# Who writes the second copy of the keys: two engines or two transfers

## The chip, the cores and the metric

The kernel runs on one core of one Trainium2 chip. The metric is the device time of one execution in microseconds (us), lower is better. Before the change the median of three runs is 1610.96 us (1610.89 to 1611.48).

## The reference, cut to what matters

Two layers of a streaming encoder (512 tokens, width 2048, everything float32). Each layer normalises `x`, projects it by one large matrix, and runs two attentions side by side:

```
h = rmsnorm(x, norm_g)
aq, ak, av, ag, bq, bk, bv, bg = split(h @ w_in)
ya = chunk_relbias_attention(aq, ak, av, rel_bias) * silu(ag)   # mixer A: 16 heads of 64, relative bias
yb = swa_sink_gqa(rope(bq), rope(bk), bv, sinks) * silu(bg)     # mixer B: 16 query heads, 2 key heads
x  = x + concat([ya, yb]) @ w_out
```

A last `rmsnorm` follows. In both mixers the scores are `q . k` over a head's 64 numbers.

## The kernel before, in words

Float32 products are made of three products of a faster format: each operand is split into a high part (`hi`, a rounding copy on ScalarE, helper L1110) and a low part (`lo`, the difference, on VectorE, helper L1581/L1582), and PE adds hi x hi, lo x hi and hi x lo (L730 to L732). Activations lie transposed, 128 columns of features by 512 tokens.

A head has only 64 features, so a pair of heads fills the 128 partitions, and half a matmul's rows would stay empty. The kernel uses them: `q_st` holds for each head the high part of the queries in its own 64 partitions and the low part in the other 64. The keys must therefore stand in both halves. `k_st` has for each of the two heads `h` a high row (`k_hi2`) and a low row (`k_lo2`), each in partitions 0 to 63 and once more in 64 to 127. Before, ScalarE writes both halves of the high part (`hi_k`, four instructions on 64 partitions) and VectorE both halves of the low part (`lo_k`, four instructions), which gives `k_done`. PE waits for `k_done` in `scores_a` (matmuls L776, L778, L779) and `scores_b` (L815).

A layer has this order. Projection tiles 0 to 3 (queries, keys, gate, values of the first pair of heads), 16 points of a quarter tile each. Then `unit_sums` for the units 1 to 7: each has 16 points, in each of which PE works off one weight place of the next pair of heads and, in between, the attention of the pair before; a loop over `u` holds the units in the middle. The first scores of a unit (`scores_a`, e = 0) stand at its point 0. The keys of the next pair are split at the points 12 (ScalarE, `HI_K_AT`) and 13 (VectorE, `LO_K_AT`) of the unit before. Then `unit` (the attention of the last pair beside the first tiles of mixer B, whose keys are split at point 12) and `phase_b` (mixer B; its first scores at point 2), and the output projection.

In `unit_sums` ten of the sixteen weight places are multiplied by a scheme that saves products (seven block products for eight) and needs differences of blocks of `h` as well: `sum_h`/`sum_last_h` make them in place in `xy`, `hi_h_sums` and `lo_h_sums` split them, five steps `m` = 0 to 4 with two instructions on each engine. Step 0 is for the fifth place, steps 1 to 4 for the first four; PE asks for them from point 1 of unit 1 on. They share memory with `xy`, so a step's high part must wait for older low parts. At the points of `H_SUMS_AT` (10 to 15 of the first 16) the steps are done.

All loads are issued by SP, in the order in which they are written, and go through one queue: `load_in` loads a weight place (256 KB) once VectorE has done the low part of the place that frees its memory; `prefetch` and L680 load whole tiles (1024 KB); `load_strips` loads the bias of a pair (two transfers, L538 and L539); `swap` exchanges rows for the rotation of mixer B (four transfers of 64 KB, L548). An instruction of SP that waits holds back all that stand behind it.

The clock of TensorE is given by the profile as a granted share of 2.4 GHz; its other level is 1.2 GHz.

Of the kernel before, what the change touches and what calls it, by code (L numbers as in the profile page):

```python
# [30 lines left out]
P = 128  # L31
# [18 lines left out]
PTS = 4  # L50
# [36 lines left out]
H_ORDER = (4, 0, 1, 2, 3)  # L87
H_SUMS_AT = (10, 11, 12, 14, 15)
SCALE_AT = {8: (0, 5), 9: (5, 7), 10: (7, 2 * IN_SUM_K)}
# [8 lines left out]
Y_BEHIND = 7  # L98
STRIPS_BEHIND = 17
SUM_AT = 6  # L100

# [34 lines left out]
def trunk(nc, xT, w, rb, sinks, gains, cos, sin, eye, flip, ext, xs, ys, out):  # L136
    with ExitStack() as ctx:
# [130 lines left out]
        k_hi_done = sem("k_hi_done")  # L268
        k_done = sem("k_done")
        swapped = sem("swapped")  # L270
        rope_cos = sem("rope_cos")
# [253 lines left out]
        def _(sp):  # L525
# [83 lines left out]
            def load_in(T, L, u, j):  # L609
# [9 lines left out]
                sp.dma_start(raw_f[:, first:first + PLAIN], rows).then_inc(in_raw[IN_PLACE[i]], 16)  # L619

            def keep_y(L, a):
                sp.wait_ge(y_done, pair_a(L, a) + 1)
                carry_wait(sp)
                sp.dma_start(ys[bass.ds(a * P, P), :], xy[:, Y_STAGE, :]).then_inc(y_kept, 16)
# [30 lines left out]
            with sp.Fori(0, DEPTH) as L:  # L655
# [6 lines left out]
                sp.wait_ge(ext_out, 16)  # L662
                load_strips(L, 0)
                for j in range(4, Y_BEHIND):
                    load_in(T, L, 1, j)
                with sp.Fori(1, PAIRS - 1) as u:
                    for j in range(Y_BEHIND, Y_BEHIND + 16):
                        load_in(T, L, u, j)
                        if j == STRIPS_BEHIND:
                            load_strips(L, u)  # L670
                    for par in range(2):
                        sp.sem_inc(w_in[par], 32)
                    keep_y(L, u - 1)
# [4 lines left out]
                for s in range(2):  # L678
                    sp.wait_ge(w_lo_done, (T + A_SLOTS) * PTS + (s - 1))
                    sp.dma_start(w_raw[:, s, :], w_v[bass.ds(T * P + (A_SLOTS + s) * P, P), :]).then_inc(w_in[s], 16)  # L680
                load_strips(L, PAIRS - 1)
                sp.wait_ge(proj_done, T + A_SLOTS)
                carry_wait(sp)
# [5 lines left out]
                sp.dma_start(xy[:, 0:PAIRS - 2, :], ys.rearrange("(t p) c -> p t c", p=P)).then_inc(y_back, 16)  # L689
                for s in range(4):  # L690
                    prefetch(T + A_SLOTS, s)
                    if s > 0:
                        swap(L, s - 1, T + (A_SLOTS + s - 1), t_q if s == 2 else t_k)
# [31 lines left out]
        def _(pe):  # L725
# [37 lines left out]
            def scores_a(g, v, e0, e):  # L763
                h, i = divmod(e, QT)
                if e == 0:
                    pe.wait_ge(q_done, g + 1)
                    pe.wait_ge(k_done, v + 1)
                if e >= 2:
                    pe.wait_ge(biased, e0 + (e - 1))
                n = (i + 1) * P  # L770
                dst = score_bank(e)[:, 0:n]
                qs = q_st[:, h, i * P:(i + 1) * P]
                if i == 0:

                    both = score_bank(e)[:, 0:2 * P].rearrange("p (w c) -> p w c", w=2)
                    pe.matmul(both, qs, k_st[:, :, h, 0:P], start=True, stop=True).then_inc(s_done, 1)  # L776
                    return
                pe.matmul(dst, qs, k_hi2[:, h, 0:n], start=True, stop=False)  # L778
                pe.matmul(dst, qs, k_lo2[:, h, 0:n], start=False, stop=True).then_inc(s_done, 1)  # L779
# [25 lines left out]
            def scores_b(L, n):  # L805
                D = n // E_B
                if n % E_B == 0:
                    pe.wait_ge(q_done, pair_b(L, 2 * D + 2))
                if n == 0:
                    pe.wait_ge(k_done, L * V_LAYER + V_LAYER)  # L810
                pe.wait_ge(biased, step_b(L, n))
                for j, c, keys in blocks(n):
                    for r in range(2):
                        dst = ps_s[j][:, r * 256:(r + 1) * 256].rearrange("p (w c) -> p w c", w=2)[:, :, 0:keys]
                        mm = pe.matmul(dst, q_b[:, r, c, :, :].rearrange("p h c -> p (h c)"),  # L815
                                       k_st[:, :, D // 2, (c + 1) * CHUNK - keys:(c + 1) * CHUNK], start=True, stop=True,
                                       skip_group_check=True)
                mm.then_inc(s_done, 1)
# [289 lines left out]
        def _(act):  # L1108
# [42 lines left out]
            def hi_k(src_ready):  # L1151
                src_ready()
                for h in range(2):
                    for half in range(2):
                        last = copy(k_hi2[64 * half:64 * half + 64, h, :], t_k[64 * h:64 * h + 64, :])
# [104 lines left out]
            def hi_h_sums(L, m):  # L1260
                if m == 0:
                    act.wait_ge(last_summed, (L + 1) * 4)
                else:
                    act.wait_ge(h_summed, (L * (IN_SUM_K - 1) + m) * 4)
                    act.wait_ge(h_sum_lo, (L * IN_SUM_K + m) * 2)
                for j in h_tiles()[2 * m:2 * m + 2]:
# [73 lines left out]

            def unit_sums(T, L, u, att, g):

                for p in range(16):
                    def other():
                        if isinstance(u, int) and p + HI_AHEAD >= 16:
                            hi_next(tile0(L) + A_SLOTS, L, p + HI_AHEAD - 16)
                        else:
                            hi_in(T, L, u, p + HI_AHEAD)
                    if p == HALF_OUT_AT[0]:
                        act.wait_ge(h_sum_lo, (L + 1) * (2 * IN_SUM_K))  # L1350
                        act.wait_ge(y_kept, L * (16 * (PAIRS - 2)) + u * 16)
                        carry_wait(act)
                    attend(att, p, Y_STAGE, other)
                    if p == TANH_AT:
                        gate(T - 2, t_gate)
# [75 lines left out]
            for L in range(DEPTH):  # L1431
# [43 lines left out]
                for s in (2, 3):  # L1475
                    for pt in range(PTS):
# [11 lines left out]
                        duties(T, L, p, ("a_first", pair_a(L, 0)))  # L1488
                with act.Fori(1, PAIRS - 1) as u:
                    unit_sums(T + u * 4, L, u, att_a(L, u - 1), pair_a(L, u))  # L1490
                unit_sums(T + (PAIRS - 1) * 4, L, PAIRS - 1, att_a(L, PAIRS - 2), pair_a(L, PAIRS - 1))
                unit(T + A_SLOTS, L, att_a(L, PAIRS - 1), ("b", None))
# [84 lines left out]
        def _(dve):  # L1577
# [36 lines left out]
            def lo_k(v):  # L1614
                dve.wait_ge(k_hi_done, v + 1)
                for h in range(2):
                    own = slice(64 * h, 64 * h + 64)
                    for half in range(2):
                        last = low(k_lo2[64 * half:64 * half + 64, h, :], t_k[own, :], k_hi2[own, h, :].bitcast(F32))
# [224 lines left out]
            def unit_sums(T, L, u, att, ab, g, v, first=False, last=False):  # L1844

                for p in range(16):
# [12 lines left out]
                    if p == 8:  # L1859
                        scale_pair(L, u, 0, QUERIES_KEYS)  # L1860
                    if p == 0 and first:
                        lo_h_sums(L, IN_SUM_K - 1)
                    if p == TURN_V_AT:
# [240 lines left out]
            for L in range(DEPTH):  # L2104
# [30 lines left out]
                for s in (2, 3):  # L2135
                    for pt in range(PTS):
                        p = s * PTS + pt
                        if p == 2 * PTS + 1:
                            presum_squares(L)
                        if p == 3 * PTS:  # L2140
                            take_rstd(L)
# [5 lines left out]
                        if p == 9:  # L2147
                            sum_last_h(L)
                        if p == 2 * PTS + 2:
                            invert_root(L)  # L2150
                        if p in H_SUMS_AT[:-1]:
                            lo_h_sums(L, H_SUMS_AT.index(p))
                dve.wait_ge(k_done, L * V_LAYER + 1)
                take(T, 3, t_v, ps=ps_t[1])
                dve.wait_ge(proj_free, T + 4)
                dve.sem_inc(rows_added, 2)
                if L < 1:
                    dve.wait_ge(const_in, 16 * N_CONST)
# [257 lines left out]
```

## Time and profile before

| | |
|---|---|
| median of 3 runs | 1610.96 us |
| profiled execution | 1612.55 us |
| its span | 1610.2 us |
| PE busy | 1589.0 us (99%) |
| VectorE (DVE) busy | 1276.6 us (79%) |
| ScalarE (ACT) busy | 954.7 us (59%) |
| GpSimd (POOL) busy | 477.5 us (30%) |
| mean granted TensorE clock | 0.993 |

The span runs from the first to the last instruction; the time around it belongs to the execution too. A row of the timeline gives start, duration, engine, line, operation, output and inputs, the count of merged instructions, and in brackets how long the engine had been idle and what ended that. PE's matmuls overlap: a matmul over 512 columns is shown with 0.39 us, while the next one starts 0.23 us later at the full clock and 0.43 us later at the lower one.

### The profile page before, as it was taken

What the parts mean: (1) busy time and instruction counts of PE and PEld (TensorE: products, weight loads), DVE (VectorE), ACT (ScalarE), POOL (GpSimd) and SP (SyncE); (2) the same over time, 40 slices, a digit from 0 to 9 for tenths busy, and PEclk for the clock granted to TensorE, in tenths of its full rate; (3) what the DMA queues carried; (4) which work ended last, traced back from release to release, by engine and by line L of the source; (5) the groups of instructions that cost most, each with busy time, mean ns of one, the idle gap of its engine ahead of it and who ended that gap; (6) DMA issues with size and microseconds to landing.
All of it is one profiled execution on the core that took longest, in us unless ns stands there. A gap on an engine that the chain in (4) does not pass through costs nothing.

```text
span 1610.2 us, 29380 instructions
## 1 busy us (share of the span) xinstructions
PE 1589.0 (99%) x9541; PEld 1418.0 (88%) x9541; DVE 1276.6 (79%) x2631; ACT 954.7 (59%) x1977; POOL 477.5 (30%) x666
## 2 busy tenths in 40 slices
PE   9899999999999999999999999999999999999997
PEld 7799999999888888899988999999988888888997
DVE  7987788887677777888878788788876787888875
ACT  7766666667556666433466666766665566663333
POOL 0754454453222100010046445445422212000000
PEclk9999999999999999999999999999999999999998
DMA  6233323323523322344432332323343233223343
GB/s 223 79 97 104 109 85 109 104 90 114 167 92 95 113 88 92 105 152 157 164 104 73 107 107 91 110 90 104 109 157 112 92 107 103 79 99 112 131 144 118
DMA packets 77511, 180.69 MB, mean 112 GB/s; under 512 B 9408, under 2 KB 13792, under 8 KB 70640
## 3 DMA queue, kind: packets, MB, share of 16 engines
q1 hardware_dynamic: 76960, 178.99, 33.3%
q8 instruction: 44, 0.72, 0.2%
q10 hardware_dynamic: 432, 0.55, 0.1%
q14 instruction: 43, 0.35, 0.1%
q0 software_dynamic: 32, 0.08, 0.0%
HBM read 163.25 MB, written 11.62 MB: 109 GB/s over the span
## 4 chain that ended last, share of the span: by engine, by line
PE 91%; DVE 6%; DMA 1%; issue 1%; ACT 1%; SPq 0%; DVEq 0%; ACTq 0%
PE ps_proj L730 10%; PE ps_proj L732 10%; PE ps_proj L731 10%; PE ps_proj L892 4%; PE ps_proj L893 4%; PE ps_proj L894 4%; PE ps_proj L905 3%; PE ps_proj L906 2%; PE ps_proj L907 2%; PE ps_o L800 2%; PE ps_t L787 2%; PE ps_s L892 2%; PE ps_s L894 2%; PE ps_s L893 2%; PE ps_t L894 2%; PE ps_t L893 2%
## 5 line engine op out<-in xcount | busy, mean ns | idle before, releaser
L1110 ACT ACTIVATE w_hi<-w_raw 128x512 fp32r<-128x512 f32 (+1 forms) x528 | 385.7, 743 | 198.5 <-DVE w_raw L1986 62.5
L1581 DVE TENSOR_TENSOR w_lo<-w_raw,w_hi 128x512 fp32r<-128x512 f32 (+1 forms) x528 | 459.4, 878 | 34.0 <-ACT w_hi L1110 29.9
L730 PE MATMUL ps_proj<-act_hi,w_hi 128*128 128x512 f32 x704 | 276.9, 393 | 0.0
L731 PE MATMUL ps_proj<-act_lo,w_hi 128*128 128x512 f32 x704 | 274.8, 390 | 0.0
L732 PE MATMUL ps_proj<-act_hi,w_lo 128*128 128x512 f32 x704 | 274.7, 390 | 0.0
L2315 POOL TENSOR_TENSOR w_raw<-w_raw 128x128 f32<-128x128 f32 x140 | 92.0, 657 | 300.1 <-DMA w_raw<-w 299.9
L732 PEld LDWEIGHTS ps_proj<-act_hi,w_lo 128*128 128x128 f32 x704 | 132.1, 188 | 28.4
L1110 ACT ACTIVATE arena<-ps_t 128x512 fp32r<-128x512 f32 (+4 forms) x168 | 75.3, 453 | 135.3 <-PE ps_t L787 82.9
L730 PEld LDWEIGHTS ps_proj<-act_hi,w_hi 128*128 128x128 f32 x704 | 132.5, 188 | 24.8
L731 PEld LDWEIGHTS ps_proj<-act_lo,w_hi 128*128 128x128 f32 x704 | 132.4, 188 | 24.3
L1175 ACT ACTIVATE probs<-probs,nmax 128x128 f32<-128x128 f32 (+3 forms) x128 | 72.1, 563 | 97.3 <-DVE nmax L1653 95.4
L1581 DVE TENSOR_TENSOR arena<-ps_t,arena 128x512 fp32r<-128x512 f32 (+4 forms) x168 | 84.6, 507 | 56.4 <-ACT arena L1110 56.0
L2279 POOL TENSOR_TENSOR temp<-temp 128x512 f32<-128x512 f32 x13 | 25.6, 1973 | 263.6 <-ACT temp L1248 263.6
L2320 POOL TENSOR_TENSOR w_raw<-w_raw 128x128 f32<-128x128 f32 x140 | 91.5, 654 | 11.0
L2317 POOL TENSOR_TENSOR w_raw<-w_raw 128x128 f32<-128x128 f32 x140 | 89.7, 641 | 11.0
L2286 POOL TENSOR_TENSOR temp<-temp,strips_tables 128x512 f32<-128x512 f32 x18 | 24.9, 1381 | 216.8 <-DVE temp L1593 216.8
L1110 ACT ACTIVATE probs<-probs,rden 128x128 f32<-128x128 f32 (+3 forms) x128 | 71.5, 558 | 28.8 <-DVE rden L1674 28.8
L2318 POOL TENSOR_TENSOR w_raw<-w_raw 128x128 f32<-128x128 f32 x140 | 79.1, 565 | 0.0
L1194 ACT ACTIVATE probs<-probs,nmax 128x128 f32<-128x128 f32 (+1 forms) x128 | 49.1, 384 | 40.5 <-DVE nmax L1667 40.5
L1653 DVE CUSTOM_DVE_ANT_0 probs<-ps_o,strips_tables 128x256 f32<-128x256 f32 x64 | 35.4, 553 | 42.8 <-PE ps_o L779 42.8
L905 PE MATMUL ps_proj<-act_hi,w_hi 128*128 128x512 f32 x168 | 67.5, 402 | 1.8 <-DVE w_lo L1581 1.8
L906 PE MATMUL ps_proj<-act_lo,w_hi 128*128 128x512 f32 x168 | 67.3, 400 | 0.0
(398 smaller groups left out, 4688.4 us busy)
## 6 DMA issues: line engine op xcount, KB each, us to landing
w_raw<-w SPq DMA_DIRECT2D x322, 256.0 KB, 3.0
w_raw<-w SPq DMA_DIRECT2D x51, 1024.0 KB, 4.9
temp<-temp SPq DMA_DIRECT2D x72, 64.0 KB, 4.0
strips_tables<-ext SPq DMA_DIRECT2D x16, 256.0 KB, 3.9
temp<-xT SPq DMA_DIRECT2D x16, 256.0 KB, 4.4
xs<-xy SPq DMA_DIRECT2D x16, 256.0 KB, 4.3
temp<-xs SPq DMA_DIRECT2D x16, 256.0 KB, 4.1
strips_tables<-ext SPq DMA_DIRECT2D x16, 224.0 KB, 4.4
```

The source lines that it names most:

```text
L730: pe.matmul(dst, wh, act_hi[:, k, :], start=start, stop=False)
L731: pe.matmul(dst, wh, act_lo[:, k, :], start=False, stop=False)
L732: return pe.matmul(dst, wl, act_hi[:, k, :], start=False, stop=stop)
L892: pe.matmul(dst, wh, hi, start=first, stop=False, skip_group_check=True)
L893: pe.matmul(dst, wh, lo, start=False, stop=False, skip_group_check=True)
L894: mm = pe.matmul(dst, in_block(lo_f, i, b), hi, start=False, stop=last, skip_group_check=True)
L905: pe.matmul(dst, hi_f[:, cols], act_hi[:, row, :], start=j == 0 and k == 0, stop=False, skip_group_check=True)
L906: pe.matmul(dst, hi_f[:, cols], act_lo[:, row, :], start=False, stop=False, skip_group_check=True)
L1110: return nc.scalar.activation(dst, src, ACT.Copy, scale=scale)
L1581: return nc.vector.tensor_tensor(dst, src, hi, ALU.subtract)
L2315: nc.gpsimd.tensor_tensor(b[S1], b[S3], b[W22], ALU.add).then_inc(in_wsum, 1)
L2320: nc.gpsimd.tensor_tensor(b[S4], b[W12], b[S2], ALU.subtract).then_inc(in_wsum, 1)
```

## The change

The engines write each head's keys only in the half of the partitions in which they already are (`half in (h,)`): two instructions in `hi_k` and two in `lo_k`. The other half is filled by `copy_k` on SP: for each head one transfer from partitions to partitions, 64 partitions by two rows of 2 KB, 256 KB in all. It waits for `k_done` and raises `k_copied`, for which PE now waits. Its calls stand behind the first strips at a layer's start, behind the load of place 20 in the loop, behind the strips of the last unit, and ahead of the fourth `prefetch` beside the last unit, for mixer B. And the splits of the sums move: step 2 on ScalarE from point 12 to 13, on VectorE from point 12 to behind the take of the values; step 3 on ScalarE stays at 14, on VectorE it goes from 14 to point 0 of unit 1; step 4 goes to point 1 of unit 1 on both. `invert_root` on VectorE moves ahead of the weight split of the same point.

```
+KEYS_BEHIND = 20
-H_SUMS_AT = (10, 11, 12, 14, 15)
+H_SUMS_AT = (10, 11, 13, 14)
+H_SUMS_AFTER = {1: 1, 3: 2, 4: 4}
...
+            def copy_k(v):
+                sp.wait_ge(k_done, v + 1)
+                carry_wait(sp)
+                for h in range(2):
+                    own, other = slice(64 * h, 64 * h + 64), slice(64 - 64 * h, P - 64 * h)
+                    sp.dma_start(k_st[other, :, h, :].bitcast(F32), k_st[own, :, h, :].bitcast(F32)).then_inc(k_copied, 16)
...
                 load_strips(L, 0)
+                copy_k(L * V_LAYER)
...
                         if j == STRIPS_BEHIND:
                             load_strips(L, u)
+                        if j == KEYS_BEHIND:
+                            copy_k(L * V_LAYER + u)
...
                 load_strips(L, PAIRS - 1)
+                copy_k(L * V_LAYER + (PAIRS - 1))
...
                 for s in range(4):
+                    if s == 3:
+                        copy_k(L * V_LAYER + PAIRS)
                     prefetch(T + A_SLOTS, s)
...
-                    pe.wait_ge(k_done, v + 1)                            # scores_a
+                    pe.wait_ge(k_copied, (v + 1) * 32)
...
-                    pe.wait_ge(k_done, L * V_LAYER + V_LAYER)            # scores_b
+                    pe.wait_ge(k_copied, (L * V_LAYER + V_LAYER) * 32)
...
-                    for half in range(2):                                # hi_k and lo_k
+                    for half in (h,):
...
                     act.wait_ge(h_summed, (L * (IN_SUM_K - 1) + m) * 4)  # hi_h_sums
-                    act.wait_ge(h_sum_lo, (L * IN_SUM_K + m) * 2)
+                if m in H_SUMS_AFTER:
+                    act.wait_ge(h_sum_lo, (L * IN_SUM_K + H_SUMS_AFTER[m]) * 2)
...
                     attend(att, p, Y_STAGE, other)                       # unit_sums, ScalarE
+                    if p == 1 and first:
+                        hi_h_sums(L, IN_SUM_K - 1)
...
-                    if p == 0 and first:                                 # unit_sums, VectorE
-                        lo_h_sums(L, IN_SUM_K - 1)
+                    if p < 2 and first:
+                        lo_h_sums(L, p + 3)
...
+                        if p == 2 * PTS + 2:                             # VectorE, ahead of split_w
+                            invert_root(L)
...
-                        if p == 2 * PTS + 2:
-                            invert_root(L)
-                        if p in H_SUMS_AT[:-1]:
+                        if p in H_SUMS_AT[:2]:
                             lo_h_sums(L, H_SUMS_AT.index(p))
...
                 dve.sem_inc(rows_added, 2)
+                lo_h_sums(L, 2)
```

## Rows read from the trace of the kernel before

**Rows 1.** Page, part 1: busy us (share of the span) x instructions.

```profile
PE 1589.0 (99%) x9541; PEld 1418.0 (88%) x9541; DVE 1276.6 (79%) x2631; ACT 954.7 (59%) x1977; POOL 477.5 (30%) x666
```

**Rows 2.** List of PE's waits: who waited for whom: total, times, longest.

```profile
PE ps_s L776 <- DVE k_st L1581: 3.7, 2, 2.5
```

**Rows 3.** Table by stage around both layer starts: busy times (instructions), then the granted clock.

```profile
56.00:66.00 10.00, 7.88 (x29) 6.00 (x28) 9.34 (x14) 5.46 (x8) 9.45 (x14) 0.83 0.12 41
846.00:862.00 16.00, 12.61 (x60) 10.42 (x59) 14.39 (x25) 10.61 (x19) 13.07 (x17) 0.79 0.15 51
```

**Rows 4.** Timeline of VectorE, ScalarE and PE at the start of layer 0.

```profile
54.61 1.70 DVE L1582 SCALAR_TENSOR_TENSOR arena<-temp,arena 64x512 fp32r<-64x512 f32 x2
56.35 3.45 DVE L1581 TENSOR_TENSOR k_st<-temp,k_st 64x512 fp32r<-64x512 f32 x4
...
52.01 1.28 ACT L1110 ACTIVATE arena<-temp 64x512 fp32r<-64x512 f32 x2
...
59.94 0.35 PE L776 MATMUL ps_s<-k_st,arena 128*128 128x256 f32 x1 [1.17 <-DVE k_st L1581]
61.24 0.50 PE L905 MATMUL ps_proj<-act_hi,w_hi 128*128 128x512 f32 x1 [0.95 <-DVE w_lo L1581]
```

**Rows 5.** The same at the start of layer 1.

```profile
847.54 3.34 DVE L1581 TENSOR_TENSOR k_st<-temp,k_st 64x512 fp32r<-64x512 f32 x4
...
843.65 1.27 ACT L1110 ACTIVATE arena<-temp 64x512 fp32r<-64x512 f32 x2
...
852.33 0.79 PE L905 MATMUL ps_proj<-act_hi,w_hi 128*128 128x512 f32 x1 [0.89 <-DVE w_lo L1581]
```

**Rows 6.** Timeline at the first and the last of twelve unit boundaries in the loop.

```profile
104.82 3.39 DVE L1581 TENSOR_TENSOR k_st<-temp,k_st 64x512 fp32r<-64x512 f32 x4
108.24 0.95 DVE L1581 TENSOR_TENSOR w_lo<-w_raw,w_hi 128x512 fp32r<-128x512 f32 x1
...
109.43 0.33 SPq L619 DMA_DIRECT2D w_raw<-w  x1
...
111.95 0.28 PE L776 MATMUL ps_s<-k_st,arena 128*128 128x256 f32 x1
...
1142.02 3.56 DVE L1581 TENSOR_TENSOR k_st<-temp,k_st 64x512 fp32r<-64x512 f32 x4
...
1149.25 0.28 PE L776 MATMUL ps_s<-k_st,arena 128*128 128x256 f32 x1
```

**Rows 7.** Transfers: KB each, us from issue to landing; strips of 343.5 to 349.5, and their issue.

```profile
w_raw<-w SPq DMA_DIRECT2D x322, 256.0 KB, 3.0
w_raw<-w SPq DMA_DIRECT2D x51, 1024.0 KB, 4.9
...
strips_tables<-ext SPq DMA_DIRECT2D x1, 256.0 KB, 3.7
strips_tables<-ext SPq DMA_DIRECT2D x1, 224.0 KB, 4.5
...
344.10 0.66 SPq L538 DMA_DIRECT2D strips_tables<-ext  x1
344.95 0.61 SPq L539 DMA_DIRECT2D strips_tables<-ext  x1
```

**Rows 8.** Last unit of layer 0: SP's second strips issue, its landing, PE's first scores.

```profile
400.81 0.61 SPq L539 DMA_DIRECT2D strips_tables<-ext  x1
...
strips_tables<-ext SPq DMA_DIRECT2D x1, 224.0 KB, 5.7
...
406.76 0.28 PE L776 MATMUL ps_s<-k_st,arena 128*128 128x256 f32 x1
```

**Rows 9.** Timeline of layer 0 before mixer B's first scores: GpSimd, VectorE, PE.

```profile
457.25 1.44 POOL L2288 TENSOR_TENSOR temp<-temp,strips_tables 128x512 f32<-128x512 f32 x1 [3.73 <-DMA temp<-temp]
...
461.74 1.39 DVE L1582 SCALAR_TENSOR_TENSOR arena<-temp,arena 64x512 fp32r<-64x512 f32 x2 [1.77 <-ACT arena L1110]
...
464.09 0.62 PE L815 MATMUL ps_s<-k_st,arena 128*128 128x128 f32 x4
```

More of the change, by code:

```diff
@@ L269, in trunk @@
         k_done = sem("k_done")
+        k_copied = sem("k_copied")
         swapped = sem("swapped")
@@ L1339, in copy_p1, with unit_sums @@
                 copy(in_w1[:, 0:SEQ // 2], in_banks(p // 8)[1][0][:, 0:SEQ // 2]).then_inc(in_copied, 1)
-            def unit_sums(T, L, u, att, g):
+            def unit_sums(T, L, u, att, g, first=False, last=False):
                 for p in range(16):
                     def other():
-                        if isinstance(u, int) and p + HI_AHEAD >= 16:
+                        if last and p + HI_AHEAD >= 16:
                             hi_next(tile0(L) + A_SLOTS, L, p + HI_AHEAD - 16)
@@ L1488, in _ @@
                         duties(T, L, p, ("a_first", pair_a(L, 0)))
-                with act.Fori(1, PAIRS - 1) as u:
+                unit_sums(T + 4, L, 1, att_a(L, 0), pair_a(L, 1), first=True)
+                with act.Fori(2, PAIRS - 1) as u:
                     unit_sums(T + u * 4, L, u, att_a(L, u - 1), pair_a(L, u))
-                unit_sums(T + (PAIRS - 1) * 4, L, PAIRS - 1, att_a(L, PAIRS - 2), pair_a(L, PAIRS - 1))
+                unit_sums(T + (PAIRS - 1) * 4, L, PAIRS - 1, att_a(L, PAIRS - 2), pair_a(L, PAIRS - 1), last=True)
                 unit(T + A_SLOTS, L, att_a(L, PAIRS - 1), ("b", None))
@@ L1617, in lo_k @@
                     own = slice(64 * h, 64 * h + 64)
-                    for half in range(2):
+                    for half in (h,):
                         last = low(k_lo2[64 * half:64 * half + 64, h, :], t_k[own, :], k_hi2[own, h, :].bitcast(F32))
```

## Prediction

> **What bounds the kernel now.** I read the page first. TensorE (PE) is busy 1589.0 of 1610.2 us [rows 1], so only some 21 us of idle time can be won, and whatever makes PE wait is paid in full. The list of PE's waits comes next: its largest entry is the first score matmul of an attention unit, L776, waiting for the split keys, 3.7 us in two waits [rows 2], and the timelines show that both are at the start of a layer. The table by stage shows what such a gap costs beside itself: the granted clock is 0.83 over 56 to 66 us and 0.79 over 846 to 862 us [rows 3]. With two levels, 2.4 and 1.2 GHz, 0.83 is 3.4 us at the lower one and 0.79 is 6.7 us. A busy PE loses half of such a time, 1.7 and 3.4 us. In the other units PE never waits for keys, so VectorE and ScalarE time that is saved there buys nothing by itself. The question is when the keys are whole: before, at the end of four VectorE instructions; after, when two transfers have landed that can start only behind two of these.
>
> **Layer starts (two).** Removed before the first score: two of four key copies on ScalarE (0.64 us each, as the query copies, 1.28/2), two of four on VectorE (3.45/4 = 0.86 each), and the split of one pair of sums (third of five) ahead of the keys on both. In layer 0 the query copy on ScalarE starts at 52.01, because it waits for the take of the queries, and ends at 53.29 (two key copies by 54.6); that does not move. VectorE is then free of the sums, so the low halves of the queries run from 53.3 to 55.0 (1.70) in place of 54.61, and two key lows of 0.86 end at 56.8 in place of 59.8 [rows 4]. In layer 1 ScalarE starts at 843.65 [rows 5], so: 844.9, 846.65, 848.4 in place of 850.9.
> SP needs about 0.2 us to see that and issue (a weight load issues 0.24 us after its releaser [rows 6]); the first copy goes out at 57.05 and 848.6. Two 256 KB transfers: one alone lands 3.0 us after its issue [rows 7]. What a second adds to a first I bound from both sides: 1024 KB land in 4.9 us, so each further 256 KB cost (4.9-3.0)/3 = 0.63; the bias strips, 64 partitions by two pieces of 2 KB like these copies, landed 3.7 us after 344.10 and 4.5 after 344.95 [rows 7], which is 5.35 us for both, behind one load. I take 1.15 us, nearer to the rows with 2 KB pieces, of which the weight places (256 KB each) are the commonest. So both are there 3.0+1.15 = 4.15 us after the first issue (3.6 to 5.35).
> The Trainium skill, page "SBUF — State Buffer", section "Door 1: The DMA port swizzle", says that 64 partitions reach only 8 of the 16 ports, some 27 GB/s each. An estimate from that page is 262144/217600 = 1.2 us for a copy, near what I took; no row here isolates it.
> Keys whole: 61.2 in layer 0, 852.75 in layer 1. Add 0.2 for the score matmul: the products start at 61.4 against 61.24 [rows 4], and 852.95 against 852.33 [rows 5]. The second wait, that for the first weights' low part (0.95 and 0.89 us), goes, because VectorE reaches them while PE still waits for the copy. Net +0.2 and +0.6 us; with the bounds -0.4 to +1.4 and +0.1 to +1.8. The idle time is now one stretch of over 4 us, where layer 0 had 1.17 and 0.95; I add one more lower-clock stretch of 3.4 us there, 1.7 us (0 to 1.7), and none in layer 1 (-1.7 to +1.7). Sum +2.5. The early reciprocal lets PE start its spread matmuls up to 1.1 us sooner, but PE then only waits longer for the keys: nothing. The later sums (two instructions each on both engines) have their cover in PE's first two or three points, each of some 3 us; if it were gone, 1.7 us each.
>
> **Inside the unit loop (12 boundaries: six in each layer).** Here the keys had slack. The four lows started at 104.82 and took 3.39, so two end at 106.5 and the score matmul is at 111.95: 5.4 us. At the last of the twelve 1142.02 + 3.56/2 = 1143.8 to 1149.25 is again 5.4 [rows 6]; the other ten lie between 5.1 and 5.6. What must fit: SP's copy stands behind the load of place 20, which waits for the next weight low on VectorE (0.7 to 0.95 us, 108.24 before), then 0.24 us until the load issues, as 109.19 to 109.43 shows. That load is 256 KB on the same queue. From its issue 3.0 us for itself and 1.15 for each copy: 5.3 us. Total 0.03+0.8+0.24+5.3 = 6.4 us against 5.4: PE waits 1.0 us. With 0.63 per transfer it is 5.3, no wait; by the strips' chain (a load 0.55 us ahead of 344.10, the last landing at 349.45, 5.9 us) it is 7.0, a wait of 1.6. I take 0.7 us, between my own 1.0 and the lower bound, since a transfer that follows another in the queue without a gap may be worth less than my 1.15. 12 x 0.7 = 8.4 us (0 to 19). A gap of 0.7 us I take to leave the clock alone: the lower clock stands in the rows only behind more than 2 us of gaps. Nothing absorbs it: ScalarE and VectorE are released by PE's own progress, so a stall of PE moves the next boundary along with it. VectorE takes up the scores' bias 2 to 3 us after the matmul, so nobody else suffers. Behind the copies in the queue stand the loads of places 21 and 22; GpSimd idles for these loads already, and the weights have more than that in hand. Removed here: 2 x 0.64 and 2 x 0.85 us per unit beside other work, worth nothing.
>
> **Unit 7 (one per layer).** The copy stands behind two 1024 KB loads and the strips. The second strips transfer issues at 400.81 and lands 5.7 us later, 406.5, with the queue full up to then; two copies behind it are there at 406.5 + 2 x 1.15 = 408.8, less perhaps 0.4. The score matmul was at 406.76 [rows 8]: a wait of 1.7 us (1.0 to 2.0), 3.4 for both layers, and possibly a lower-clock stretch of 1.7 each, which I leave to the range.
>
> **The keys of mixer B (one per layer).** The copy now stands ahead of a 1024 KB load and of the swap of queries for the rotation. The load is issued some 6 us later, and the swaps come to lie behind 1.5 MB. VectorE gives the queries 1.4 us sooner. GpSimd took up the swapped rows at 457.25, after which ScalarE and VectorE finish the queries at 461.74+1.39 = 463.1, and the scores follow at 464.09 [rows 9]. I find the swaps landing about when they did. Nothing, with 0 to 2 us in the range.
>
> **Sum.** 2.5+8.4+3.4 = +14.3 us. The profiled execution took 1612.55 us, 2.35 over its span, and would take 1626.8; it stands 1.6 us above the median of 1610.96, which I carry over unchanged: 1625.2.
>
> **Rivals.**
> 1. *The transfers are there in time.* At 0.63 us per further 256 KB the twelve boundaries cost nothing; the mechanism is the same queue at the rate of the large loads. For it: the row of 1024 KB in 4.9 us. Against: these are 8 KB pieces and the copies 2 KB. The layer starts give -0.4 and +0.1, unit 7 costs 2 x 1.0: +1.7, so 1612.7. It decides from a wait-free boundary when both copies land within 4.3 us of the load's issue.
>  The Trainium skill, page "DMA: Bandwidth & Descriptors", section "Anatomy of one DMA", has a fixed 2.0 us and bytes/436 GB/s. An estimate by it gives 2.0+1.8 = 3.8 us for the load and both copies, so by that rule too no boundary would wait.
> 2. *Not slower but faster.* The two copies run beside each other and land 3.3 us after issue. Then products start at 60.5 and 852.1 (-0.7 and -0.2), PE loses no more than it does, and if one lower-clock stretch in each layer goes with the second gap, 3.4 us more are won; unit 7 takes back 0.8: -3.5, so 1607.5. For it: keys 2.5 to 3 us sooner on VectorE is real. Against: the gap stays longer than 2 us even so.
> 3. *Slow copies.* The strips' pace everywhere: 12 x 1.6 + 2 x 2.0 + (1.4+1.8+1.7) = +28, so 1639; if the clock also fell at each stall, over 1650.
> 4. That the copies don't halve the engines' work is excluded by the loop over `(h,)`: eight instructions a unit become four.
>
> **Chances and range.** Forecast 0.52, its own range 1618 to 1634; rival 1 0.22, rival 2 0.11, rival 3 0.15. 0.2% is 3.2 us, about what a measurement of this kernel can tell from no change. Slower: 0.52+0.15 and a third of rival 1, 0.74; same: most of the rest of rival 1, 0.15; faster 0.11. The range, 1609 to 1638, leaves out most of rival 2 and the tail of rival 3.
>
> **What would show it.** In the profile after: PE's wait at the first score matmul has a DMA of the keys as its releaser, 16 times; 12 of them near 0.7 us, unit 7's near 1.7, those at the layer starts 4 to 5; no wait of PE for the first weight low. Key lows end near 56.8 and 848.4. The copies land 4.2 us after the first issue at a layer start and 4.7 in the loop. I am wrong if the loop's boundaries show no wait, or if layer starts get shorter.

## The result, and the profile after

The changed kernel takes 1647.13 us (median of 4 runs, 1645.01 to 1647.98), the kernel before 1611.22 us beside it on the same chip (1610.89 to 1611.56): a ratio of 1.0222, 95% interval 1.0209 to 1.0234. It is slower, and by some 36 us where the forecast had 14; the time lies above the range, of which 1638 was the upper end. The profiled execution took 1646.77 us, its span is 1644.5 us against 1610.2.

The page of the kernel after, part 1 as in [rows 1], then the line of the copies from part 6:

```profile
PE 1596.7 (97%) x9541; PEld 1419.9 (86%) x9541; DVE 1246.0 (76%) x2595; ACT 923.5 (56%) x1931; POOL 472.9 (29%) x666
...
k_st<-k_st SPq DMA_DIRECT2D x36, 256.0 KB, 4.1
```

VectorE and ScalarE are relieved of 30.6 and 31.2 us, as promised (36 and 46 instructions fewer; e1 below shows that ten of ScalarE's 46 are not the keys'). PE's share falls from 99% to 97%. The copies land a median of 4.1 us after their issue. The list of PE's waits, with the columns of [rows 2], says where PE stood:

```profile
PE ps_s L793 <- DMA k_st<-k_st: 31.5, 16, 5.5
PE ps_s L832 <- DVE arena L1603: 3.0, 2, 1.5
```

L793 is the old L776, the first scores of a unit: 3.7 us in two waits on VectorE have become 31.5 us in sixteen waits on a DMA of the keys, one in every unit. L832 is the first scores of mixer B, waiting for the rotated queries, a wait that was not there.

The timeline of the kernel after, in the order layer start (0, then 1), first loop boundary, sixth loop boundary, last unit (0, then 1):

```profile
55.25 1.71 DVE L1602 TENSOR_TENSOR k_st<-temp,k_st 64x512 fp32r<-64x512 f32 x2
57.05 1.33 SPq L630 DMA_DIRECT2D k_st<-k_st  x2
61.65 0.58 PE L793 MATMUL ps_s<-k_st,arena 128*128 128x256 f32 x1 [5.54 <-DMA k_st<-k_st]
...
870.09 0.58 PE L793 MATMUL ps_s<-k_st,arena 128*128 128x256 f32 x1 [4.47 <-DMA k_st<-k_st]
...
105.88 1.82 DVE L1602 TENSOR_TENSOR k_st<-temp,k_st 64x512 fp32r<-64x512 f32 x2
107.73 0.83 DVE L1602 TENSOR_TENSOR w_lo<-w_raw,w_hi 128x512 fp32r<-128x512 f32 x1
109.35 1.31 SPq L630 DMA_DIRECT2D k_st<-k_st  x2
113.15 0.39 PE L924 MATMUL ps_t<-act_hi,w_lo 128*128 128x512 f32 x1
114.80 0.38 PE L793 MATMUL ps_s<-k_st,arena 128*128 128x256 f32 x1 [1.27 <-DMA k_st<-k_st]
115.03 0.49 PE L922 MATMUL ps_proj<-act_hi,w_hi 128*128 128x512 f32 x1
115.36 0.39 PE L923 MATMUL ps_proj<-act_lo,w_hi 128*128 128x512 f32 x1
...
368.55 0.38 PE L793 MATMUL ps_s<-k_st,arena 128*128 128x256 f32 x1 [1.39 <-DMA k_st<-k_st]
...
412.71 1.30 SPq L630 DMA_DIRECT2D k_st<-k_st  x2
420.77 0.36 PE L793 MATMUL ps_s<-k_st,arena 128*128 128x256 f32 x1 [2.79 <-DMA k_st<-k_st]
...
1229.64 0.36 PE L793 MATMUL ps_s<-k_st,arena 128*128 128x256 f32 x1 [3.03 <-DMA k_st<-k_st]
```

The lows end at 56.96, the copy goes out at 57.05, and PE waits. At the loop's boundary the lows end at 107.70, the next weight low at 108.56, the load of place 20 goes out at 108.80 and the copies at 109.35. The transfers issued there, each with the us from its own issue to its landing (the list of transfers, windows of 0.6 us around 108.8, 109.4 and 110.0):

```profile
w_raw<-w SPq DMA_DIRECT2D x1, 256.0 KB, 3.6
k_st<-k_st SPq DMA_DIRECT2D x1, 256.0 KB, 4.1
k_st<-k_st SPq DMA_DIRECT2D x1, 256.0 KB, 4.7
```

The load lands at 112.45, the first copy at 113.47 and the second, issued at 110.04, at 114.76; the score matmul starts 0.04 us behind it. The twelve waits at such boundaries lie between 0.99 and 1.64 us and sum to 15.6, 1.30 each.

A wait costs more than the gap that is shown. In the kernel before, PE's first scores of the sixth boundary stand at 357.70, five periods of 49.15 us behind 111.95 [rows 6]. Behind that first one stand two matmuls that are shown here too:

```profile
112.06 0.40 PE L905 MATMUL ps_proj<-act_hi,w_hi 128*128 128x512 f32 x1
112.30 0.40 PE L906 MATMUL ps_proj<-act_lo,w_hi 128*128 128x512 f32 x1
...
357.70 0.28 PE L776 MATMUL ps_s<-k_st,arena 128*128 128x256 f32 x1
```

After, 114.80 to 368.55 is five periods of 50.75 us: 1.60 more in each, 1.65 in layer 1 (from 923.58 to 1177.15, against 245.31 us before), some 0.3 us over the gap of 1.30. At the first boundary the whole of it can be seen. The matmul at 113.15 is shown with 0.39 us, but in full flow the next would have started 0.23 us after it, as the rows of the kernel do; counted from there the wait is 1.42. And PE takes two matmuls to get back into its flow: from the scores to the next matmul and from that to the one behind it go 0.23 and 0.33 us, where it was 0.11 and 0.24 before. 1.42 and 0.21 are 1.63. This I call the restart.

The table by stage of the kernel after (columns as in [rows 3]) around the two layer starts, one loop boundary and a last unit:

```profile
56.00:68.00 12.00, 6.46 (x21) 5.19 (x21) 9.64 (x17) 6.92 (x11) 11.30 (x18) 0.72 0.39 111
866.00:882.00 16.00, 11.91 (x64) 10.80 (x65) 11.67 (x23) 9.55 (x17) 8.86 (x13) 0.79 0.36 104
100.00:118.00 18.00, 16.73 (x104) 14.83 (x104) 14.33 (x24) 8.75 (x15) 12.72 (x20) 1.00 0.45 133
409.00:427.00 18.00, 15.21 (x73) 12.71 (x72) 12.29 (x26) 6.04 (x13) 0.00 (x0) 0.91 0.81 240
```

A gap of 1.27 us leaves the clock at 1.00. Behind the gap of 2.79 us it is 0.91 over 18 us: with levels of 1 and 0.5 that is 3.2 us at the lower one, 1.6 us lost beside the gap. Around the layer starts it is as forecast: 0.72 over 12 us is 6.7 us at the lower level in layer 0, where the 0.83 over 10 us of [rows 3] was 3.4, and in layer 1 0.79 stays 0.79.

### The profile page after: what moved, and what is told of

The parts are those of the page before. It is cut to its first block, busy times and chain, and to the rows that moved or that the text cites. A ratio compares the mean times of both kernels' runs of the same rounds, so it can differ in the third digit from the quotient of the medians.

```text
span 1644.5 us, 29305 instructions
## 1 busy us (share of the span) xinstructions
PE 1596.7 (97%) x9541; PEld 1419.9 (86%) x9541; DVE 1246.0 (76%) x2595; ACT 923.5 (56%) x1931; POOL 472.9 (29%) x666
## 4 chain that ended last, share of the span: by engine, by line
PE 81%; DVE 7%; DMA 5%; issue 3%; ACT 1%; SPq 1%; POOL 1%; DVEq 0%; POOLq 0%; ACTq 0%
PE ps_proj L749 9%; PE ps_proj L747 9%; PE ps_proj L748 9%; DMA k_st<-k_st 5%; PE ps_proj L909 3%; PE ps_proj L911 3%; PE ps_proj L910 3%; PE ps_proj L922 3%; PE ps_proj L923 2%; PE ps_proj L924 2%; PE ps_t L804 2%; DVE w_lo L1602 2%; PE ps_s L909 2%; PE ps_s L911 2%; PE ps_s L910 2%
```

## The experiments

Theory Q: the time comes from where the copies stand in SP's queue and how long two half-tile copies take behind a load. Rivals: the later sums cost or bring something; the traffic itself disturbs loads and engines; the copies are slow for their 2 KB pieces, or for using one queue. The kernel before was run on the same chip each time (medians 1610.9 to 1611.2).

**e1_sums_only: the later sums alone**, on the kernel before, both engines writing both halves. The edit is the part of the diff that moves the sums and `invert_root`, without `copy_k`.

> Only the second part of the change: the splits of the sums later and the reciprocal earlier; both engines write both halves of the keys, no copies, TensorE waits for k_done as before. Theory Q (the whole loss is TensorE waiting for the second copy to land, at 16 places, plus mixer B): this part is free and even gains, since the key lows end 1.2 us (layer 0) and 0.8 us (layer 1) sooner and the products of unit 1 follow; 1606 to 1610 us, the key wait at the layer starts shorter, the one before the spread matmuls near 1.0 in place of 2.2. Rival S (the moved sums collide with the first points of unit 1): 1614 or more, with waits of TensorE for h_sum at the points 2 to 4.

Measured: 1611.57 us (10 runs), ratio 1.0003 (0.9993 to 1.0012). PE's waits:

```profile
PE ps_s L778 <- DVE k_st L1587: 5.9, 2, 3.3
```

The keys are whole at 58.99 in place of 59.80, but PE arrives earlier still and waits 5.9 us in place of 3.7. A gain was expected and there is none: what the later sums bring PE ahead of the first scores, it gives back there.

**e2_copy_only: the copies alone**, on the kernel before.

```
-                    for half in range(2):        # hi_k and lo_k
+                    for half in (h,):
-                    pe.wait_ge(k_done, v + 1)
+                    pe.wait_ge(k_copied, (v + 1) * 32)
```

with `copy_k` and its calls as in the change.

> Only the first part: the transfers make the second copy, the sums stay where they were before. Theory Q: same waits in the loop (12 x 1.3), unit 7 (2 x 2.9) and mixer B; at the layer starts the keys are 1.7 to 2 us later than in the changed kernel, so 1650 to 1653 us. Rival S: without the moved sums the time falls, to 1645 or less.

Measured: 1649.96 us (4 runs), ratio 1.0240 (1.0223 to 1.0258); PE's waits on the copies are 32.3 us in 16. So the whole slowdown is the copies', and it lies a hair under the 1650 to 1653 expected.

**e3_copy_earlier: the copy one place earlier in the queue**, so that it doesn't stand behind the load of place 20.

```
-KEYS_BEHIND = 20
+KEYS_BEHIND = 19
```

> The changed kernel with KEYS_BEHIND 19 in place of 20: in the loop the copies stand ahead of the load of place 20 and start as soon as the keys are done, 1.65 us sooner and with no load ahead of them. Theory Q: second copy lands 4.6 us after the first issue (as it does at the layer start, 57.05 to 61.61), that is 4.8 us after the key lows, against 5.4 available: the 12 waits vanish, 12 x 1.6 = 19 us less, 1626 to 1630 us. Rival T (the traffic itself slows the weights' loads): the gain is under 8 us, since the load of place 20 now stands behind 512 KB and GpSimd and ScalarE get it later; TensorE then waits for w_lo.

Measured: 1624.80 us (4 runs), ratio 1.0084 (1.0067 to 1.0101): one digit gives back 22.3 us of the change's 35.9. It was expected at 1626 to 1630 and came out 1.2 us below. PE's waits of this kernel, its queue and first scores at the first loop boundary, and the table by stage there and at the last unit of layer 1:

```profile
PE ps_s L793 <- DMA k_st<-k_st: 14.9, 4, 5.5
PE ps_s L832 <- DVE arena L1603: 2.3, 2, 1.3
```

```profile
107.23 1.31 SPq L630 DMA_DIRECT2D k_st<-k_st  x2
113.01 0.28 PE L793 MATMUL ps_s<-k_st,arena 128*128 128x256 f32 x1
```

```profile
100.00:118.00 18.00, 18.00 (x117) 16.45 (x117) 14.14 (x25) 9.18 (x16) 12.79 (x20) 1.00 0.46 131
1204.00:1222.00 18.00, 15.75 (x75) 12.77 (x75) 9.90 (x25) 7.20 (x18) 0.00 (x0) 1.00 0.67 214
```

All twelve waits of the loop are gone. The copies go out at 107.23 instead of 109.35, land 3.2 and 3.8 us after their issues, at 110.44 and 111.69, and PE starts at 113.01 without a gap; the weight load goes out at 108.87 against 108.80 and loses nothing. Time falls by 22.3 us. The waits on the copies fall by 16.6, of which 15.6 are the loop's and 1.0 the last units', and mixer B's wait by 0.7; 12 x 0.33 = 4.0 more are the restarts. What is left, 1.0 us, may be the clock: in this execution it doesn't fall in the last unit of layer 1, behind a gap of 2.25 us.

**e4_dry: the traffic without the wait.** Both engines write both halves, PE waits for `k_done`, and the copies go at the same place, in the same size, to a buffer in memory that nobody reads.

```
-                    sp.dma_start(k_st[other, :, h, :].bitcast(F32), ...
+                    sp.dma_start(k_dry[other, :, :], ...
-                    pe.wait_ge(k_copied, (v + 1) * 32)
+                    pe.wait_ge(k_done, v + 1)
```

> The changed kernel, but both engines write both halves again and TensorE waits for k_done; the copies are still issued at the same places and of the same size, into a DRAM tensor that nobody reads. It prices the transfers alone: SP's time, the queue, the loads behind them. Theory Q: nothing in the loop, at most 1 to 3 us at mixer B (the swaps lie behind the copies): 1608 to 1613 us. Rival T: 1620 or more, with TensorE waiting for w_lo in the loop or for strips.

Measured: 1620.97 us (4 runs), ratio 1.0062 (1.0046 to 1.0079), 8 us above the range that was expected. PE's longest wait:

```profile
PE ps_s L833 <- DVE arena L1604: 7.4, 2, 4.0
```

The loop and the last units show no wait, as Q has it. But the scores of mixer B wait 7.4 us: the queue alone costs there. This is the copy standing ahead of a load of 1024 KB, and the load ahead of the row swaps for the rotation. That it is more than the 3.0 us of the changed kernel fits the copy's issue: behind four lows in place of two it goes out 1.7 us later beside PE's work, and all behind it too.

**e5_mixer_engines: e3, and mixer B's keys by both engines again**, its `copy_k` removed.

> The copy-earlier kernel (KEYS_BEHIND 19, measured 1624.8 us) with the keys of mixer B written in both halves by the engines again, without a copy. Theory Q says that the copies there hold back the 1024 KB load and the swaps behind it, and through them the queries: the two waits of TensorE at the first scores of mixer B (1.0 and 1.3 us) vanish, about 3 us less with the restarts: 1621 to 1622.5 us. Rival: they come from the later k_done or from other timing and stay: 1624 to 1625.

Measured: 1621.41 us (4 runs), ratio 1.0064 (1.0047 to 1.0081), and L832's wait is gone from the list: 3.4 us less than e3. For the mechanism compare, before [rows 9], SP's swaps at 452.01 and the load at 444.88 (the queue's timeline of the kernel before),

```profile
444.88 0.34 SPq L529 DMA_DIRECT2D w_raw<-w  x1
452.01 2.41 SPq L548 DMA_DIRECT2D temp<-temp  x4
```

with the kernel after:

```profile
465.14 1.33 SPq L630 DMA_DIRECT2D k_st<-k_st  x2
466.75 0.42 SPq L532 DMA_DIRECT2D w_raw<-w  x1
467.49 3.75 SPq L551 DMA_DIRECT2D temp<-temp  x4
475.97 1.28 POOL L2310 TENSOR_TENSOR temp<-temp,strips_tables 128x512 f32<-128x512 f32 x1 [8.45 <-DMA temp<-temp]
```

The load that stood 7.1 us ahead of the swaps now stands 0.7 us ahead, since it has to wait behind the copy for the keys, and the copies of 512 KB stand there as well. The four swaps land a median of 5.4 us after their issues in place of 2.0, before and after:

```profile
temp<-temp SPq DMA_DIRECT2D x4, 64.0 KB, 2.0
```

```profile
temp<-temp SPq DMA_DIRECT2D x4, 64.0 KB, 5.4
```

GpSimd gets the swapped rows 8.5 us after the first swap's issue, where it was 5.2. How much of this is the load's and how much the copies' e5 doesn't tell, for it takes both away; e8 below says that both count.

**e9_starts_only: e5, and the last unit's keys by both engines too.**

> The copy-earlier kernel (KEYS_BEHIND 19) with both halves by the engines at mixer B and in unit 7: copies at the two layer starts and in the loop. It splits the 10.4 us between the kernel without mixer B's copy (1621.4) and the one with copies in the loop alone (1611.0). Theory Q by the waits: unit 7 costs its two waits of 2.4 us and two restarts of 0.3, 5.4 us; the layer starts the rest, 5: 1615.5 to 1616.5 us. Rival C: the long idle time at a layer start drops the clock for longer and the starts cost 8 or more: 1619.

Measured: 1613.62 us (10 runs), ratio 1.0012 (1.0003 to 1.0022): 7.8 us less than e5, for 4.7 us less of waits (14.6 in 4 became 9.9 in 2). The rest is the clock. 400 to 418 us of e5, then of this kernel:

```profile
400.00:418.00 18.00, 15.50 (x66) 12.50 (x66) 11.20 (x25) 6.76 (x16) 0.00 (x0) 0.91 0.90 279
```

```profile
400.00:418.00 18.00, 18.00 (x90) 15.21 (x89) 14.19 (x32) 8.04 (x18) 0.00 (x0) 1.00 0.72 233
```

0.91 of 18 us is 1.6 us lost, 3.2 in both layers, and 4.7 + 3.2 = 7.9. The expectation gave the last units 5.4 us, waits and restarts without the clock, and the time came out 2 us below its range.

**e6_loop_only: e9, and the layer starts by the engines too**; the copies are left only in the loop, ahead of the load of place 20.

> As the last, but the engines write both halves at the layer starts and in unit 7 as well: copies only in the loop, 12 of them, ahead of the load of place 20. Theory Q: no wait of TensorE for a copy is left, and the engines' time that is saved is worth nothing since TensorE never waited for them there: the same as before within 0.2%, 1609 to 1613 us. Rival E (relief of ScalarE and VectorE is worth something): 1605 or less. Rival T (traffic costs): 1616 or more.

Measured: 1611.01 us (10 runs), ratio 0.9997 (0.9988 to 1.0007). The layer starts' copies cost 2.6 us, give or take some 2. And the idea at its best, 24 instructions gone from each engine (VectorE busy 1251.3 us, ScalarE 928.6) and no wait for a copy, is worth nothing.

**e7_pieces_4k: the change with pieces of 4 KB.** `k_st` is laid out head first, so that a copy is 64 pieces of 4 KB instead of 128 of 2 KB.

```
-        k_st = sb("k_st", [P, 2, 2, SEQ], F32R)
+        k_raw = sb("k_st", [P, 2, 2, SEQ], F32R)
+        k_st = k_raw[:, :, :, :].rearrange("p h a c -> p a h c")
```

> The changed kernel (copies behind the load of place 20) with k_st laid out so that a head's high and low row stand next to each other: each copy moves 64 pieces of 4 KB in place of 128 of 2 KB, the same bytes between the same partitions. If the slow step between transfers (1.0 to 1.3 us per 256 KB against 0.63 for loads with 8 KB pieces) comes from the small pieces, the second copy lands 4.5 to 4.8 us after the first issue in place of 5.4 and each of the 16 waits shrinks by 0.6 to 0.9: 1634 to 1638 us. If it comes from a transfer reading and writing only 64 partitions, nothing changes: 1645 to 1648.

Measured: 1646.95 us (4 runs), ratio 1.0222 (1.0201 to 1.0243), waits 33.7 us in 16. The small pieces are not what makes the copies slow.

**e10_two_queues: e5, with the second head's copy issued by ScalarE**, at the same moment as SP's.

> The kernel without mixer B's copy (KEYS_BEHIND 19, 1621.4 us) with the second head's copy issued by ScalarE on its own queue at the same moment as the first by SP. In one queue the second lands 1.25 us after the first (60.0 and 61.3). If that step is the queue's order, both now land about 3.3 to 3.7 us after the issue and the wait at a layer start falls from 5.5 to 4.5. If the 16 DMA engines are what is shared, both land together at about 4.4 us and nothing is won; ScalarE then only loses the issue time: 1620 to 1623.

Measured: 1622.96 us (2 runs), ratio 1.0072 (1.0054 to 1.0091), against 1621.41 for e5. At the first loop boundary SP issues at 107.19 and ScalarE at 107.20, and the transfers take:

```profile
k_st<-k_st SPq DMA_DIRECT2D x1, 256.0 KB, 3.4
k_st<-k_st ACTq DMA_DIRECT2D x1, 256.0 KB, 4.9
```

Issued together on two queues the last lands at 112.05, 4.86 us after the issue; in e5, with one queue, it is 4.53 (107.31 to 111.84). At the other places outside the last units it is 4.5 to 5.2 with two queues, once 3.7, and 4.4 to 4.6 with one. So the order of one queue isn't the limit either.

**e8_high_first: the high parts' copies ahead of the load, the low parts' behind it**, each two transfers of 128 KB, and high before low at all other places.

```
                         if j == KEYS_BEHIND - 1:
+                            copy_part(L * V_LAYER + u, 0, k_hi_done)
                         if j == KEYS_BEHIND:
-                            copy_k(L * V_LAYER + u)
+                            copy_part(L * V_LAYER + u, 1, k_done)
```

> The changed kernel with the copies cut by high and low part in place of one per head: the high parts (2 x 128 KB) are issued before the load of place 20 as soon as ScalarE has made them, the low parts (2 x 128 KB) behind it. Half of the bytes are out of the way when the keys are done. If bytes in the queue set the landing, the last lands about 1.2 us sooner, waits in the loop of 0.1 to 0.3 us: 1628 to 1634 us with all 16 places. If issues set it (four of 0.6 us each in place of two), little is won: 1640 or more.

Measured: 1616.66 us (6 runs), ratio 1.0033 (1.0020 to 1.0045), the best with all sixteen copies, and better than expected. PE's waits on the copies:

```profile
PE ps_s L799 <- DMA k_st<-k_st: 11.0, 5, 3.8
```

Only half of the bytes are left once the lows are ready, so even behind the load the last copy is there at 111.41, before PE. At the layer starts the waits are 3.83 and 2.78 us, at the last units 2.02 and 2.21. Mixer B's scores don't wait either, though the load of 1024 KB stands 0.7 us ahead of the swaps here too (452.76 and 453.45); only 256 KB of copies are left in front of it, and GpSimd has the rows 6.4 us after the first swap's issue:

```profile
459.86 1.30 POOL L2316 TENSOR_TENSOR temp<-temp,strips_tables 128x512 f32<-128x512 f32 x1 [6.07 <-DMA temp<-temp]
```

**b1_lows_by_act: another way for the layer starts.** e1, where VectorE makes the low part of each head once and ScalarE copies it to the other half; no transfer. ScalarE also makes the high part of the weights of place 0 ahead of the sums'.

> A version without transfers: the sums split later, and at the two layer starts alone ScalarE copies the other half of the low keys from VectorE's own half (2 x 0.64 us, the first beside VectorE's second low) in place of two lows of 0.86 on VectorE; the weights of place 0 go ahead of the sums on ScalarE. The keys are whole at 58.2 in place of 59.0 (sums alone) and 59.8 (before), VectorE is free 1.7 us sooner for the first weight low. 1 to 1.5 us less per layer: 1608 to 1610 against 1611. If VectorE's other work fills the place, the same as before.

Measured: 1609.12 us (11 runs), ratio 0.9986 (0.9977 to 0.9995), as expected.

**b2_products_first: b1, and PE multiplies unit 1's first weight place ahead of the first scores**, so that it works while the keys are split.

> The last version, and TensorE multiplies place 0 of unit 1 before the unit's first scores (the other units as before); the first weight low goes ahead of the key lows. TensorE then has 2.7 us of work while the keys are split, which covers most of the gap of 3.3 and 2.6 us: 1605 to 1608 us. Rival: VectorE is full here and the low part of place 1, or the turn of the first scores at point 2, comes late instead: 1609 to 1612, with waits of TensorE for w_lo or probs.

Measured: 1608.62 us (11 runs), ratio 0.9985 (0.9976 to 0.9994); just above the range expected and not told apart from b1. The clock, 56 to 68 and 846 to 862 us, of b1 and then of b2 (with 66 to 72 us too), and b2's waits:

```profile
56.00:68.00 12.00, 9.50 (x44) 8.17 (x45) 9.79 (x18) 9.36 (x15) 11.00 (x18) 0.72 0.15 50
846.00:862.00 16.00, 14.05 (x84) 12.21 (x83) 13.31 (x24) 13.06 (x23) 9.45 (x15) 0.89 0.21 67
```

```profile
56.00:68.00 12.00, 7.04 (x43) 5.87 (x42) 9.40 (x16) 9.64 (x16) 11.36 (x17) 0.99 0.13 44
66.00:72.00 6.00, 4.63 (x25) 4.64 (x26) 5.89 (x11) 4.36 (x11) 2.78 (x3) 0.72 0.23 76
846.00:862.00 16.00, 12.11 (x79) 10.88 (x78) 13.07 (x24) 13.28 (x24) 11.28 (x16) 1.00 0.16 52
```

```profile
PE ps_proj L895 <- DVEq L2190: 4.9, 2, 2.8
PE ps_t L790 <- ACT probs L1117: 3.8, 2, 2.0
```

In layer 1 the clock stays up; in layer 0 it falls later and for less time, 0.72 over 66 to 72 us. The waits are split and moved to the next weight place and to the first turned probabilities; the likely reason is that VectorE and ScalarE have the same work to do as before. Both are some 0.15% below the kernel before, with intervals that just leave out no change; they are the fastest here.

## Why the prediction was wrong

Where the slowdown lies, beside the terms of the sum. By the runs: each run takes one place away from the one before it, and the waits by which the last units and mixer B got shorter in e3 are counted with them and not with the loop. By the traces: PE runs the same 9541 matmuls in the same order before and after, so at any matmul the lag of the later trace behind the earlier one can be read, and its growth over each place is given.

| place | forecast | by the runs | from | by the two traces |
|---|---|---|---|---|
| 12 loop boundaries | 8.4 | 20.6 | e3's 22.3 less 1.0 and 0.7 | 19.7 (9.6 and 10.0) |
| last units | 3.4 | 8.8 | e5 to e9, 7.8, and 1.0 of waits | 9.5 (4.6 and 4.9) |
| mixer B's keys | 0 | 4.1 | e3 to e5, 3.4, and 0.7 of waits | 3.6 (1.7 and 1.8) |
| layer starts | 2.5 | 2.6 | e9 to e6 | 2.3 (1.3 and 0.9) |
| elsewhere | 0 | | | -1.3 |
| sum | 14.3 | 36.1 | measured as a whole 35.9 | 33.7 |

**The mechanism was right.** PE's wait at the first scores has the DMA as its releaser sixteen times; the key lows end at 56.96 for 56.8; the load of place 20 goes out 1.10 us after the lows for 0.03+0.8+0.24 = 1.07. The copies land 4.56 us after the first issue in layer 0 for 4.15, the first alone taking 3.3 and not 3.0. The layer starts cost what was forecast, the added lower-clock stretch in layer 0 included; that 2.6 meets 2.5 so closely is luck, with 2 us of uncertainty between the two runs. The later sums and the early reciprocal give nothing (e1), nor does the engines' time in the loop (e6).

**The step that failed is the term of the unit loop, "From its issue 3.0 us for itself and 1.15 for each copy: 5.3 us".** At the first boundary it measured 5.96. The load takes 3.65 us, not 3.0, with two copies behind it, and the copies add 1.02 and 1.29. The 1.15 was sized right; wrong was to put it behind a load priced alone. The rows held a better answer: the strips' chain, the only one with a load ahead and half-tile transfers behind, gave 5.9 and a wait of 1.6, and I kept it as the upper bound. Then I shaved my own 1.0 to 0.7 "since a transfer that follows another in the queue without a gap may be worth less", with no row for it. The waits were 1.30 for 0.7, and each costs 1.63, for PE doesn't restart at full flow; the sum had no term for that. (With a chain longer by 0.66 us the wait would be 1.7; it is 1.4 from PE's flow, since PE came 5.7 us behind the lows, 107.70 to 113.38, and not 5.4.) Together 11 to 12 of the missing 21.6 us.

**The last units:** 1.7 us of wait was forecast, 2.79 and 3.03 came, for the same reason (the strips and two copies are one chain of half-tile transfers: in layer 0 the second strips land 6.5 us after their issue where the sum had 5.7, and the copies behind them 6.7 and 7.3 us after theirs), and the clock fell as well, "a lower-clock stretch of 1.7 each, which I leave to the range": it came in both layers, 3.4 us in all, and belonged in the sum. Together 5 to 6 us.

**Mixer B:** "I find the swaps landing about when they did" is wrong. The prediction saw it coming, "The load is issued some 6 us later, and the swaps come to lie behind 1.5 MB", and priced it at nothing without a row for it. The swaps land 5.4 us after their issue in place of 2.0, more than the 1.4 us by which VectorE gives the queries sooner. 3.4 to 4.1 us, and e4 shows that it needs no wait on the copy at all. Load and copies both count: with half of the copies' bytes gone ahead and the load in the same place PE doesn't wait (e8).

**The rivals.** Rival 3 had the right pace of the queue in the loop, 5.9 us for 5.96, and came nearest with 1639, still 8 us too low, for it had mixer B and the last units low. That its 1.6 us a boundary meet the 1.63 is luck: it priced the gap alone, and the gap is 1.30. Rival 1, transfers in time, is excluded: it needed both copies within 4.3 us of the load's issue. The fixed 2.0 us plus bytes/436 GB/s that the Trainium skill gives, page "DMA: Bandwidth & Descriptors", section "Anatomy of one DMA — SWDGE (gpsimd) path", would be 3.8 us for the load and both copies, an estimate by a fit that the page gives for transfers issued by GpSimd. These are issued by SP, and 5.96 was measured; the measurement decides. Rival 2, copies beside each other, is excluded by the layer starts, where the second lands 1.29 us behind the first, and by e10.

**Why a copy costs 1.2 to 1.3 us where a full-width 256 KB adds less** isn't its pieces (e7) nor the order of one queue (e10). The second copy lands 1.29 us behind the first, as a rate 262144 bytes at 203 GB/s. The Trainium skill, page "SBUF — State Buffer", section "Door 1: The DMA port swizzle", says that 64 partitions reach 8 of 16 ports; the 196 GB/s that it reports for partitions 0 to 63 at 1 MiB, and its limit of about 218, lie on either side of that rate. But a step between landings isn't the time of the bytes. At mixer B's keys the two copies start with the queue empty, and e4 has the same copies there into memory. The packets of all transfers in the 2.4 us in which the copies move (466.4 to 468.8 after the change, 451.6 to 454.0 in e4) are given by one and the same line in both:

```profile
DMA packets 295, 0.58 MB, mean 242 GB/s; under 512 B 32, under 2 KB 32, under 8 KB 288
```

Both pairs of copies, 0.52 MB of it, are through in the same time, yet the second lands 1.17 us behind the first in the one kernel and 0.98 in the other; after the change its last 2 KB end at 468.79 and it lands at 469.61. Over all places the step is 1.1 to 1.7 us between the halves and 0.7 to 1.05 into memory. So part of it comes after the bytes, and it depends on where they go. No run here varies the partitions of a transfer; that the ports are the cause is argued, not shown, and these rows don't support it.

What stays open: the two columns differ by up to 1 us at a place. A stretch at the lower clock, 1.7 us, comes in some executions and not in others, as in the last unit of layer 1 in e3, and there is one profile of each kernel.

## What to carry to other kernels

A transfer's place in the queue can matter more than the transfer: here one place earlier in the same queue was worth 22 us of 36. Price a chain of transfers by the nearest chain in the trace that has as many in front of it and the same partitions, not by adding single landings, and where such a row stands among the bounds, take it. On the engine that bounds the kernel a periodic wait costs its gap, the restart, and where it is long the clock; and work taken off engines that weren't awaited was worth nothing, 24 instructions on each of two.

## What the runs showed of the hardware

- A 256 KB load that lands 3.0 us after its issue as the median takes 3.4 to 3.7 with two copies issued behind it (3.65 at the first boundary, where the same load took 3.0 before), and 3.3 just behind two copies (e3). What follows in the queue counts, not only what stands ahead.
- Copies between halves of the partitions: 3.3 us for the first of 256 KB with nothing ahead, 1.1 to 1.3 more for the second, with pieces of 2 or 4 KB; issued at one moment on two queues the last lands no sooner than on one (4.5 to 5.2 us for 4.4 to 4.6, once 3.7); 3.0 us each at 128 KB (e8). From the same partitions into memory the second adds 0.7 to 1.05 (e4), though the packets of both take the same 2.4 us.
- A gap of PE of 1.3 us costs 1.6, with the clock at 1.00. In the last unit the clock is 0.91 over 18 us behind gaps of 2.5 to 3.0 us, and once behind 2.1 (e5); behind 2.25 (e3) it stays at 1.00, and behind 2.0 and 2.2 in e8. In e7 it is 0.91 over 18 us once in the loop too, behind a gap of 1.85 us.
